# Expert up products with both halves of the rows in one stationary tile, a part of w1 in fp32, and seven places for split pieces

## The reference

```python
xb = x_pad[slot_tok].reshape(nb, MOE_BLOCK, D)
def run_block(args):
    xblk, e = args
    hid = jax.nn.silu(xblk @ w1[e]) * (xblk @ w3[e])
    return hid @ w2[e]
yb = lax.map(run_block, (xb, block_e)).reshape(P, D)
y = jnp.zeros((T + 1, D), jnp.float32).at[slot_tok].add(yb * slot_w[:, None])[:T]
```

## Time and profile before

| | us |
|---|---|
| median of 3 runs (1912.04 to 1912.63) | 1912.3 |
| the profiled execution | 1909.9 |
| its span, first to last instruction | 1908.1 |
| loop of the expert blocks, about | 1340 to 1900 |
| mean granted TensorE clock | 0.945 |

### The profile page before, as it was taken

One profiled execution on the slowest core, in us unless ns is written; L12 is line 12 of the kernel. 1 busy time (PEld: TensorE's weight loads), 2 busy tenths in 40 slices (PEclk: granted clock), 3 DMA queues, 4 the chain that ended last, 5 costly groups with the idle time before them and its releaser, 6 DMA issues.

```text
span 1908.1 us, 22953 instructions
## 1 busy us (share of the span) xinstructions
PE 1723.3 (90%) x7380; PEld 1250.9 (66%) x7380; DVE 1142.3 (60%) x1525; ACT 894.8 (47%) x1196; POOL 845.0 (44%) x443
## 2 busy tenths in 40 slices
PE   2899999989998989989689998884999999999996
PEld 2788888777775877458578467672555665666664
DVE  5676673634133265335663314226899999999996
ACT  3544452522323321122422133331788888888885
POOL 0588884242432333113202032110577666776674
PEclk9899999999999999999769998985999999999998
DMA  8343453221321442322104232131899999999994
GB/s 287 99 133 100 121 172 133 95 88 50 101 81 44 155 166 96 125 94 85 38 0 130 88 133 89 44 132 53 311 368 357 374 375 374 372 386 383 378 375 161
DMA packets 135405, 340.92 MB, mean 179 GB/s; under 512 B 14580, under 2 KB 66044, under 8 KB 110504
## 3 DMA queue, kind: packets, MB, share of 16 engines
q1 hardware_dynamic: 127938, 320.69, 46.5%
q0 software_dynamic: 5200, 8.41, 2.0%
q10 hardware_dynamic: 2198, 10.92, 1.5%
HBM read 329.75 MB, written 18.87 MB: 183 GB/s over the span
## 4 chain that ended last, share of the span: by engine, by line
PE 57%; DVE 12%; POOL 12%; issue 11%; ACT 4%; DMA 2%; DVEq 1%; POOLq 0%; ACTq 0%; SPq 0%
PE ps L690 14%; PE ps L692 13%; PE ps L691 13%; PE ps L662 10%; POOL parts L2254 9%; PE ps L672 3%; POOL out L2276 2%; DVE arena L1508 2%; ACT arena L1379 2%; DVE arena L2149 1%; PE ps L1010 1%; PE ps L895 1%; PE ps L1011 1%; PE ps L868 1%; DMA arena<-in_x 1%
## 5 line engine op out<-in xcount | busy, mean ns | idle before, releaser
L2222 POOL TENSOR_TENSOR parts<-ring,parts 128x1024 fp32r<-128x1024 f32 x150 | 372.8, 2491 | 793.4 <-ACT parts L1057 790.2
L1349 ACT CAST parts<-ring 128x1024 fp32r<-128x1024 f32 x384 | 396.2, 1048 | 95.2 <-PE ps L692 71.0
L690 PE MATMUL ps<-parts,act_parts 128*128 128x512 f32 (+2 forms) x1088 | 428.7, 394 | 10.5 <-POOL parts L2254 4.0
L692 PE MATMUL ps<-parts,act_parts 128*128 128x512 f32 (+2 forms) x1088 | 423.9, 390 | 0.0
L691 PE MATMUL ps<-parts,act_parts 128*128 128x512 f32 (+2 forms) x1088 | 423.0, 389 | 0.0
L2045 DVE TENSOR_TENSOR parts<-ring,parts 128x1024 fp32r<-128x1024 f32 x289 | 396.7, 1423 | 26.8 <-ACT parts L1349 20.8
L1057 ACT CAST parts<-ring 128x1024 fp32r<-128x1024 f32 x150 | 155.5, 1047 | 384.6 <-PE ps L692 295.7
L2254 POOL TENSOR_TENSOR parts<-ring,parts 128x1024 fp32r<-128x1024 f32 x95 | 261.0, 2748 | 147.6 <-ACT parts L1349 146.7
L690 PE MATMUL ps<-act_parts,parts 128*128 128x512 f32 x640 | 253.1, 395 | 10.2 <-DVEq L1635 6.0
L692 PE MATMUL ps<-act_parts,parts 128*128 128x512 f32 x640 | 251.0, 392 | 0.0
L691 PE MATMUL ps<-act_parts,parts 128*128 128x512 f32 x640 | 251.0, 392 | 0.0
(11 more groups left out here) (250 smaller groups left out, 1890.6 us busy)
## 6 DMA issues: line engine op xcount, KB each, us to landing
ring<-in_w SPq DMA_DIRECT2D x192, 1024.0 KB, 7.4
ring<-in_w_in SPq DMA_DIRECT2D x30, 1024.0 KB, 7.3
ring<-in_w_in SPq DMA_DIRECT2D x34, 512.0 KB, 5.3
ring<-in_w_ada SPq DMA_DIRECT2D x12, 1024.0 KB, 14.3
ring<-in_w_ret_out SPq DMA_DIRECT2D x8, 1024.0 KB, 6.2
ring<-in_w_out SPq DMA_DIRECT2D x8, 1024.0 KB, 10.2
ring<-in_w_in SPq DMA_DIRECT2D x16, 256.0 KB, 4.1
gates_dram<-arena ACTq DMA_DIRECT2D x8, 512.0 KB, 5.5
```

Source lines behind the costliest of these rows:

```text
L690: pe.matmul(o, lhs[1], rhs[0], start=start, stop=False)
L692: return pe.matmul(o, lhs[0], rhs[0], start=False, stop=stop)
L1349: act.copy(parts[:, n % 4, 0, :], ring[:, j, n % 4 * 1024:(n % 4 + 1) * 1024]).then_inc(piece_hi, 1)
L2222: pool.tensor_tensor(parts[:, g % 4, 1, :], ring[:, st.place(j), k * 1024:(k + 1) * 1024], parts[:, g % 4, 0, :].bitcast(F32), ALU.subtrac ...
```

## The change

- `xg_whole` holds the first four of the eight 128-wide slices of the turned rows in fp32, with zeros beside them (128 stationary columns). The first half of w1 (pieces 0 and 1) is multiplied straight from `ring` by four fp32 products. Those two pieces are no longer split, and TensorE itself releases that half of the ring.
- The other twelve slices of w1 and w3 take two products each in place of three: the high and low rows are stacked as 128 stationary columns (`xgT` is laid out anew). The result is then in two halves of the bank, so for w1 and for w3 there is a copy of the lower 64 rows by ACT (`low_up`) and an addition in place by DVE (`add_low`). The sigmoid waits for the first addition.
- The ten pieces that are left have seven places: 2 to 8 in the first seven, 9 to 11 in the first three again. The casts therefore wait for other events.
- ACT's order becomes: high 2, 3, low_rows, high_hidden, high 4 to 7, low_up of w1, high 8, sigmoid, high 9, 10, low_up of w3, high 11, high_rows (now two copies). DVE's: low 2, low_hidden, add_rows, low 4, 5, 6, add_low of w1, low 8, gate, low 9, 10, add_low of w3, hidden, rest. POOL's stays.
- SP loads w1's second half before its first.

```diff
+WHOLE = 2
+PER_BLOCK = 12 - WHOLE
...
+        more_parts = act_parts[:, 2048:8192].rearrange("p (s h n) -> p s h n", s=3, h=2)
+        def piece_parts(n):
+            s = n - WHOLE if n < WHOLE + 7 else n - WHOLE - 7
+            return parts[:, s] if s < 4 else more_parts[:, s - 4]
...
-                for n in range(2):
+                for n in (0, 1) if j else (1, 0):
...
+                    for n in range(whole):
+                        for t in (2 * n, 2 * n + 1):
+                            mm = pe.matmul(o, xg_whole[:, t].rearrange("p h s -> p (h s)"), ring[:, 0, t * 512:(t + 1) * 512],
+                                           start=t == 0, stop=False)
+                        mm.then_inc(piece_split[n], 1)
...
-                            mm = split_product(o, hi_lo(xgT[:, :, t, :]), hi_lo(parts[:, n, :, c * 512:(c + 1) * 512]),
-                                               t == 0, t == KT - 1)
+                            rows = xgT[:, t].rearrange("p h s -> p (h s)")
+                            pe.matmul(o, rows, w[:, 0, c * 512:(c + 1) * 512], start=t == 0, stop=False)
+                            mm = pe.matmul(o, rows, w[:, 1, c * 512:(c + 1) * 512], start=False, stop=t == KT - 1)
...
             with act.Fori(0, act.snap(steps - 1)) as r:
-                up("moe", r + 2, 0, r + 1, ends=("moe", 5, r))
+                high(2, r + 2, used=(9, r))
+                high(3, r + 2, used=(10, r))
                 low_rows(r)
                 high_hidden("moe", r)
-                up("moe", r + 2, 4, r + 1, ends=("moe", 1, r + 1))
-                down(r + 1)
+                high(4, r + 2, ends=("moe", 5, r))
+                for n in (5, 6):
+                    high(n, r + 2, used=(n, r + 1))
+                high(7, r + 2, ends=("moe", 2, r))
+                low_up("moe", 0, r + 1)
+                high(8, r + 1, used=(8, r))
+                gate("moe", r + 2, r + 1)
+                high(9, r + 1, used=(2, r + 2))
+                high(10, r + 1, ends=("moe", 1, r + 1))
+                low_up("moe", 1, r + 1)
+                high(11, r + 1, used=(4, r + 2))
                 high_rows("moe", 0, r + 1)
...
+            def add_low(stage, j, b, i=0):
+                dve.wait_ge(up_low_ready, b * 2 + (1 + j))
+                o = full(stage, 1 + j, i)[0:SLOTS, :]
+                moe(dve.tensor_tensor(o, o, up_low[j][0:SLOTS, :], ALU.add))
+                moe.wait()
+                if j == 0:
+                    dve.nop().then_inc(up_sum_ready, 1)
...
             with dve.Fori(0, dve.snap(steps - 1)) as r:
-                moe.enter(r, 4)
-                for n in (0, 1, 2):
-                    low(n, r * 12 + (20 + n))
+                moe.enter(r, 6)
+                done = r * PER_BLOCK + (first + PER_BLOCK)
+                lows((2,), done)
                 low_hidden("moe", r + 1, r)
                 add_rows(r)
-                for n in (4, 5, 6):
-                    low(n, r * 12 + (20 + n))
+                lows((4, 5, 6), done)
+                add_low("moe", 0, r + 2, r + 1)
+                lows((8,), done)
                 gate("moe", r + 2, r + 1)
-                for n in (8, 9, 10):
-                    low(n, r * 12 + (20 + n))
+                lows((9, 10), done)
+                add_low("moe", 1, r + 2, r + 1)
                 hidden("moe", r + 2, r + 1)
```

More of the change, by code:

```diff
@@ L370, in build @@
         y_low = carve([D])
+        up_low = [carve([FF]) for _ in range(2)]
+        xg_whole = carve([2 * WHOLE, 2, SLOTS])
         block_w = carve([2 * MT, 64])
@@ L1340, in _, with after @@
                 take("h3T", t, h3T[:, t, :], done=h3T_ready)
+            def after(n, rounds):
+                each, used = (DOWN_USED, down_used) if n in DOWN_USED else (UP_USED, up_used)
+                return used, rounds * len(each) + each.index(n) + 1
             def high(n, block, used=None, ends=None):
@@ L1347, in high @@
                 elif used is not None:
-                    act.wait_ge(moe_used[n % 4], used)
-                act.copy(parts[:, n % 4, 0, :], ring[:, j, n % 4 * 1024:(n % 4 + 1) * 1024]).then_inc(piece_hi, 1)
+                    act.wait_ge(*after(*used))
+                act.copy(piece_parts(n)[:, 0, :], ring[:, j, n % 4 * 1024:(n % 4 + 1) * 1024]).then_inc(piece_hi, 1)
             for g in range(len(PIECE_CHUNK) - 4, len(PIECE_CHUNK)):
                 piece_released(act, g)
-            for n in range(4):
+            for n in range(WHOLE, 4):
                 high(n, 0)
@@ L1366, in high_rows, with low_up, gate @@
             def high_rows(stage, k, i=0):
[L1367 to L1374, removed]
+                o = full(stage, k, i).rearrange("p (t n) -> p t n", t=KT)
+                act.copy(xg_whole[:, :, 0, :], o[:, 0:2 * WHOLE, :]).then_inc(xgT_hi, 1)
+                act.copy(xgT[:, :, 0, :], o).then_inc(xgT_hi, 1)
+            def low_up(stage, j, i=0):
+                act.copy(up_low[j][0:SLOTS, :], full(stage, 1 + j, i)[SLOTS:2 * SLOTS, :]).then_inc(up_low_ready, 1)
+            def gate(stage, b, i=0):
+                act.wait_ge(up_sum_ready, b + 1)
+                act.activation(sg_h[0:SLOTS, :], full(stage, 1, i)[0:SLOTS, :], ACT.Sigmoid).then_inc(sg_h_ready, 1)
             def low_rows(c):
@@ L1403, in _ @@
             high_hidden("moe", act.snap(steps - 1))
-            for n in range(3):
-                high(8 + n, steps, used=pieces["moe"].before(n, steps))
+            for n in (8, 9, 10):
+                high(n, steps, ends=("moe", 5, act.snap(steps - 1)))
             high(11, steps, ends=("moe", 5, act.snap(steps - 1)))
@@ L2044, in low @@
                 dve.wait_ge(piece_hi, done + 1)
[L2045 to L2050, removed]
+                dve.tensor_tensor(piece_parts(n)[:, 1, :], ring[:, n // 4, n % 4 * 1024:(n % 4 + 1) * 1024],
+                                  piece_parts(n)[:, 0, :].bitcast(F32), ALU.subtract).then_inc(piece_split[n], 1)
+            low(2, 0)
             o = full("route", 1)
@@ L2121, in _ @@
             dve.nop().then_inc(slots_ready, 1)
+            own(dve.memset(xg_whole, 0.0))
             for c in range(2 * MT):
```

108 lines of the change are left out of this document (66 added, 42 removed).

## The result

The changed kernel takes **1982.8 us** (median of 4 runs, 1979.4 to 1986.2) against 1912.5 for the one before on the same chip (4 runs): a ratio of 1.036, interval 1.0339 to 1.0381. The forecast was 1929.5, within 1889 to 1987. So the sign was right and the time is inside the range, but +70 us came where +17 was forecast, and 1982.8 is what rival A was priced at (1984).

A forecast was written before the change was run, and what follows sets the result against it. Bound: POOL and DVE taking turns at splits, with DVE's queue setting 18.2 us per block. 1909.9 + 20.6 (29 blocks) - 3.5 (first blocks) = 1927, plus 2.4 for the median: 1929.5 us, range 1889 to 1987.

The forecast's parts named there:

- rival A: Expert loop: POOL first at both places, piece 11 before DVE's 10 and 3 before 2; 20.1 us per block, 1984; chance 0.26.
- What bounds, and the turns: Expert loop: POOL and DVE splits take turns at a shared port pair; 17.3 us per block before, 15.0 after.
- Who asks first, first pair: After POOL's piece 7: POOL asks for piece 11 at 2.91 to 2.96 us, before DVE's piece 10 at 3.04.
- third pair: DVE's piece 6 against POOL's piece 7: the prediction had piece 7 follow DVE's pieces 4, 5, 6, adding 2.35 us.
- The second pair: DVE's piece 2 against POOL's piece 3: both ask at 8.93 us, a draw; DVE taken as first.
- The price of the forecast's own order: Loop with POOL before piece 10, DVE before piece 3: 18.2 us per block against 17.49, +20.6 us; chance 0.31.
- The middle of what the draw can give: Reason for choosing 18.2 us per block: the middle if the tie of pieces 2 and 3 falls now one way, now the other.
- Rival B: Expert loop: DVE's piece 10 goes before POOL's piece 11; 16.9 us per block, 1892 us; chance 0.28.
- C: Rival: DMA is the bound; transfers keep the old pace, 17.3 to 17.4 us per block, 1904 to 1909; chance 0.09.
- D: Clock rival: PE idles 2 to 4 us per block, granted clock falls to 1.2 GHz; 1940 to 2010 us; chance 0.06.
- First blocks: Pieces 4 to 7 of block 0 cast without waiting on PE, `up` 2 us shorter: -3.5 us (bounds 0 and -7).
- PE's and DVE's terms: Per block: PE net -2.0 us (-2.75 fewer products, +0.76 fp32); DVE net -0.6 (two splits less, two additions more).

The follow-up runs named there:

- gate_late: Changed kernel with DVE's gate moved behind piece 10 instead of between pieces 8 and 9: 1934.2 us, ratio 1.0132 to the kernel before.
- rows_first: Changed kernel with ACT's two high_rows copies ahead of the cast of piece 11 instead of behind it: 1903.6 us, ratio 0.9964 to the kernel before.
- gate_first: Changed kernel with DVE's gate back before piece 8, as in the kernel before: 1882.4 us, ratio 0.9855 to the kernel before.

## Why the prediction was right or wrong

- **What bounds, and the turns: right.** Every quoted hold-up of DVE is a split standing until 1.08 to 1.10 behind the end of POOL's, and with POOL's splits left out none takes over 1.23. Who is first can't always be read from the starts (gate_late's piece 2). `add_low` reads and writes PSUM, takes 0.68 and doesn't hold POOL up: POOL's piece 7 ends 2.58 behind DVE's split with an addition beside it (1509.41 less 1506.83) and 2.60 without one (gate_late, 1603.66 less 1601.06).
- **Who asks first, first pair: right, with its size.** 2.91 to 2.96 against 3.04 forecast, 2.89 against 3.05 measured, and POOL is first in 27 of the last 30 blocks. The three others go to the third pair, which the prediction took as settled (piece 7 asked behind piece 6).
- **The second pair: wrong, and this is the step that failed.** The prediction called it a draw, 8.93 each, and took "DVE before piece 3" as forecast. Measured are 8.88 for POOL and 9.07 for DVE. DVE's 0.14 are two entries of its sum: `add_low` to the weighted product 0.84 instead of 0.80, and from there to `rest` 1.24 instead of the 1.12 of the earlier trace rows; the idle time before `rest` is 0.50 now, 0.39 then. That row had been taken over to a list in which the operation follows another one, and why the idle time grew by 0.11 isn't settled. Where two requests lie 0.0 us apart by a sum of ten rows, the forecast should have been read from what each side's errors can do; all the likely ones (one more wait, an operation with new neighbours) were on DVE's side. Rival A should have been the likeliest.
- **The price of the forecast's own order: too low, the second fault.** Where DVE is first at piece 2, the block isn't 18.2 us. The nearest case in the changed kernel is decided by 0.01 us:

```profile
1397.82 1.22 DVE L2097 TENSOR_TENSOR parts<-ring,parts 128x1024 fp32r<-128x1024 f32 x1
1399.57 0.42 DVE L2195 TENSOR_TENSOR act_parts<-ps,act_parts 128x256 fp32r<-128x256 f32 x1 [0.53 <-ACT act_parts L1394]
```

```profile
1397.83 3.44 POOL L2323 TENSOR_TENSOR parts<-ring,parts 128x1024 fp32r<-128x1024 f32 x1 [0.74 <-ACT parts L1379]
```

From the end of piece 7 to that of the next are 18.99 us. `low_hidden` waits 0.53 for ACT, a term that the prediction has at nothing, so piece 4 starts at 12.86 and not 12.4, and piece 7 is longer, as below. In most of the nine blocks with piece 2 free the period is 19.4 to 19.5. By the prediction's own sum 19.0 a block makes about 1953 us, outside its range of 1921 to 1938: the draw falling its way would not have saved the number.

- **Rival A: right** in order, in piece 2 (3.25, forecast 3.5) and nearly in the period (20.33 where all is steady, forecast 20.1). The 0.2 are mostly in one term, POOL's piece 7. The prediction counts 2.35 from 0.08 before piece 6's end; by that count it takes 2.66 (2.58 behind the end), +0.31, and the rest gives back 0.07. The mean of the last 29 is 19.95, since in 9 of them piece 2 comes first after all; 29 x 2.46 = 71.
- **"The middle of what the draw can give"** had no basis: a block costs 20.3 with piece 2 held up and mostly 18.9 to 19.5 with it free, and what a kernel costs is how often it falls which way.
- **Rival B, the other side:** not what happened, but its price was near: rows_first has its order at 17.33 a block, gate_first piece 10 first too, by more, at 16.4 (B had 16.9). **C** showed as a floor only once the order was mended; for its 17.3 to 17.4 a block the prediction's sum gives 1903 to 1906 and not 1904 to 1909. **D:** the dips are there, but the blocks of 20.33 are no longer for them.
- **First blocks:** -3.5 forecast; -0.6 before the first mark and -1.7 in the first period are there, then +1.6 in the second, and -1.4 behind the last mark, which I had at nothing.
- **PE's and DVE's terms** stand: in gate_first's order the new data path runs a block in 16.4 us where the old one needs 17.4. What the change saves is real, and its new order on DVE spends it more than three times over: gate_first differs from the changed kernel by the place of one line and by 5.05 points of the ratio, 97 us.

## What to carry to other kernels

Where two engines take turns at something, write down for each pair of requests when each side asks, and by how much the first one wins. Each pair that falls wrong costs 2 to 3.5 us here. A margin of 0.2 us held in the run (the first pair, 0.16, fell the same way in all 27 blocks that had it), but it is too small to forecast from a sum of ten rows, and where both sides wait for the same event, as the copy and piece 4 do for `add_rows`, 0.01 us decides. An edit that moves one small operation on one engine moves all the pairs behind it. Put operations that need no turn (the gate here), and above all those that wait for somebody, where the other engine holds the turn anyway. Judge such an edit together with the orders next to it: a change that saves work on every engine can lose 3.6%, and the same work in another order can win 1.5%.

## What the runs showed that I had not expected

- A longer wait can be a gain: POOL waiting 4.22 us instead of 2.90 for ACT, and the kernel 76 us faster (0.0396 of 1911).
- Gains from order don't add: 0.9964 and 0.9855 alone, 1.0052 together. The periods then repeat over four blocks (17.9, 17.9, 19.9, 16.4).
- POOL's copy of 64 indices takes 0.18 us or up to 1.27, by when a split of DVE ends; 1.19 at 1607.12 and 0.18 at 1613.15 in the earlier trace rows. So the small copy is in the turns as well, and decides the third pair.
- POOL's piece 7 in the changed kernel ends 2.6 us behind DVE's split; in the block of the earlier trace rows it was 2.27 (1618.95 less 1616.68). It is written to another tile now, but that isn't why: the kernel before has 2.6 as well, in its nine blocks of about 17.7. There, as in the changed kernel, POOL's record for issuing the scatter still runs when piece 7 starts; in the blocks with 2.27 it has ended 0.2 before. POOL, then DVE (whose third split ends at 1387.93), in the kernel before:

```profile
1386.61 1.50 POOL L2276 DMA_INDIRECT out<-arena,idx_out  x1 [0.91 <-POOL idx_out L2273]
1387.66 2.88 POOL L2254 TENSOR_TENSOR parts<-ring,parts 128x1024 fp32r<-128x1024 f32 x1
```

```profile
1384.43 3.50 DVE L2045 TENSOR_TENSOR parts<-ring,parts 128x1024 fp32r<-128x1024 f32 x3 [0.42 <-ACT parts L1349]
```
